# Softmax attention in a hybrid attention layer: heads taken one at a time, against pairs of heads on half arrays of TensorE

## The reference, cut to what matters

```python
# SWA (branch B, window 128, sink), WIN (branch A, window 512): banded_attention
s = einsum("bnqhgd,bnkhd->bnhgqk", qb, kw) * Dh ** -0.5 - slopes * rel     # window mask
p = masked_softmax(s, mask, sink);  o = einsum("bnhgqk,bnkhd->bnqhgd", p, vw)
# SEL (branch A, all 16 blocks of 64 keys are taken, so it is causal attention): sel_block
sc = einsum("bqhd,bqkd->bhqk", qi, kg) * scale - slopes * d
pr = masked_softmax(sc, d >= 0);        o = einsum("bhqk,bqkd->bqhd", pr, vg)
y_A = g0 * o_cmp + g1 * o_sel + g2 * o_win
# FGT (block two): forgetting_attention
logits = einsum("bhqd,bhkd->bhqk", qi, k32) * scale + ci - c               # causal mask
o = einsum("bhqk,bhkd->bhqd", softmax(logits), v)
```

## Time and profile before

| | |
|---|---|
| median of 3 runs | 2864.52 us (2863.51 to 2866.34) |
| the profiled execution | 2866.92 us, its span 2864.9 us |
| mean granted clock of TensorE | 0.951 of full |
| PE busy | 2675.0 us, 93% of the span, 12580 matmuls |
| DVE, ACT, POOL busy | 923.5, 818.3, 873.8 us |

### The profile page before, as it was taken

How to read it: one execution, slowest core, us unless ns; L and a number is a source line. 1 busy time by engine, 2 the same in 40 slices (tenths; PEclk the granted TensorE clock), 3 DMA queues, 4 the chain that set the end, 5 groups by cost and what they waited for, 6 DMA issues and landing times.

```text
span 2864.9 us, 30315 instructions
## 1 busy us (share of the span) xinstructions
PE 2675.0 (93%) x12580; PEld 2132.9 (74%) x12580; DVE 923.5 (32%) x1435; ACT 818.3 (29%) x1219; POOL 873.8 (31%) x492
## 2 busy tenths in 40 slices
PE   7799999999998999999998999698999999999896
PEld 5677778666686777787876777487888888888785
DVE  5213440233302544411147465504122222222423
ACT  4102441344322444422222333223211111111321
POOL 2112212444322111144632121234333232333633
PEclk8889999999998999999989999899999999999898
DMA  7001101100011000011212000120111111111111
GB/s 290 30 23 43 33 29 45 37 19 19 15 51 54 10 19 17 8 47 43 103 73 67 16 23 17 33 97 29 51 45 52 45 45 51 52 51 45 50 37 68
DMA packets 34440, 134.84 MB, mean 47 GB/s; under 512 B 3648, under 2 KB 4096, under 8 KB 32896
## 3 DMA queue, kind: packets, MB, share of 16 engines
q1 hardware_dynamic: 33984, 131.85, 13.3%
q10 hardware_dynamic: 320, 1.05, 0.1%
HBM read 123.45 MB, written 8.39 MB: 46 GB/s over the span
## 4 chain that ended last, share of the span: by engine, by line
PE 88%; DVE 5%; ACT 3%; POOL 2%; issue 2%; DMA 0%; POOLq 0%; SPq 0%; ACTq 0%; DVEq 0%
PE slot L659 55%; PE slot L705 12%; PE ps L887 4%; PE ps L858 3%; PE ps L836 2%; PE ps L737 2%; PE ps L920 1%; PE ps L911 1%; PE ps L924 1%; PE ps L937 1%; DVE cacc L2097 1%; PE ps L780 1%; POOL wlo L1500 1%; PE ps L763 1%; ACT zs L1226 0%
## 5 line engine op out<-in xcount | busy, mean ns | idle before, releaser
L659 PE MATMUL slot<-xhi,whi 128*128 128x512 f32 x2192 | 716.0, 408 | 57.6 <-ACT zs L1226 16.9
L659 PE MATMUL slot<-xlo,whi 128*128 128x512 f32 x2192 | 693.4, 398 | 0.0
L659 PE MATMUL slot<-xhi,wlo 128*128 128x512 f32 x2192 | 689.6, 396 | 0.0
L1500 POOL TENSOR_TENSOR wlo<-raw,whi 128x1024 fp32r<-128x1024 f32 (+1 forms) x169 | 429.0, 2539 | 835.1 <-ACT whi L1134 835.1
L659 PEld LDWEIGHTS slot<-xhi,whi 128*128 128x128 f32 x2192 | 406.5, 194 | 146.6 <-issue 65.3
L659 PEld LDWEIGHTS slot<-xlo,whi 128*128 128x128 f32 x2192 | 421.7, 192 | 92.2
L659 PEld LDWEIGHTS slot<-xhi,wlo 128*128 128x128 f32 x2192 | 421.3, 192 | 92.5
L1134 ACT ACTIVATE whi<-raw 128x1024 fp32r<-128x1024 f32 (+1 forms) x169 | 186.1, 1101 | 317.7 <-PE slot L705 174.1
L705 PE MATMUL slot<-uhi,whi 128*128 128x512 f32 x512 | 158.3, 390 | 0.0
L705 PE MATMUL slot<-ulo,whi 128*128 128x512 f32 x512 | 157.8, 389 | 0.0
L705 PE MATMUL slot<-uhi,wlo 128*128 128x512 f32 x512 | 157.6, 389 | 0.0
(11 more groups left out here) (315 smaller groups left out, 3079.1 us busy)
## 6 DMA issues: line engine op xcount, KB each, us to landing
raw<-wstream SPq DMA_DIRECT2D x129, 512.0 KB, 3.3
raw<-wstream SPq DMA_DIRECT2D x40, 640.0 KB, 3.9
ada<-wada SPq DMA_DIRECT2D x7, 1024.0 KB, 19.9
mm<-xT SPq DMA_DIRECT2D x2, 2048.0 KB, 9.8
ada<-wada SPq DMA_DIRECT2D x2, 2048.0 KB, 27.2
mm<-xT SPq DMA_DIRECT2D x8, 512.0 KB, 4.5
res_dram<-mm SPq DMA_DIRECT2D x8, 512.0 KB, 3.0
res<-res_dram SPq DMA_DIRECT2D x8, 512.0 KB, 6.7
```

The source lines that it names most:

```text
L659: o = mm_(outs[:, half * HALF:(half + 1) * HALF], w[b % 2][:, k_w, :], x[:, k_x, half * HALF:(half + 1) * HALF], start=first and j == 0, s ...
L1500: tt(flat(wlo[b % 2])[:, 0:n], (raw1 if b == 1 else raw)[:, 0:n], flat(whi[b % 2])[:, 0:n].bitcast(F32), ALU.subtract).then_inc(w_lo, 1)
```

## The change

Units become 64 **pairs**: heads 2t and 2t+1 for one block of queries (`pair`). The pair's keys are worked in pieces of at most 4 blocks (88 pieces in all). The queries of SEL, WIN and FGT come in the order 0, 7, 1, 6, 2, 5, 3, 4.

- Scores: head 0 of the pair on array rows 0 to 63 into the first bank of `ps4`, head 1 on rows 64 to 127 into the second, in turns. A second piece waits until the bias of the first has left the banks.
- DVE: bias for each head, one maximum over both heads, one factor for both, and now a multiplication of the exponentials by the factor before they are transposed (two `tensor_scalar` in `factor`, up to 128x1024 each).
- Product with V: V (64 columns) as weights, the transposed probabilities (128 columns) as the moving side; head 0 on array columns 0 to 63, head 1 on 64 to 127. The result has features on partitions and goes by one copy or addition to `yfm`. So `ytrans` is gone for A, B and FGT.
- The event `soft` is split into finer ones; only one pair is ahead of another: two buffers `ring` instead of three.
- `cmp` events weigh 1.0 and pauses 2.5 (10 pauses), where they weighed 2.0 and 5.0 beside heavier units; the last `cmp` step uses column groups too, and its gate is multiplied into the probabilities before.
- Retention: scores of even heads in one bank, of odd heads in the other, no `ordered`, no alternation.

```diff
+SOFT_WEIGHT = {"scores": 0.18, "turn_p": 0.12, "values": 0.28}     # times the piece's blocks
 def weight(ev):
-    if ev[0] == "soft":
-        u, first, n = ev[1:]
-        return 1.5 + sum(0.5 * unit(v)[4] for v in (u, u - 2) if first <= v < first + n)
+    if ev[0] in SOFT_WEIGHT:
+        return SOFT_WEIGHT[ev[0]] * piece(ev[1], ev[-1])[1]
+    if ev[0] in ("bias", "exp", "factor", "qsplit", "ksplit"):
+        return 0.0
...
+QORDER = (0, 7, 1, 6, 2, 5, 3, 4)
...
 def soft_events(first, n):
...
+    def scores(p):
+        rows = [("row", p, a) for a in range(2)] if pair(p)[0] == "FGT" and pair(p)[2] == 0 else []
+        return rows + [ev for c in range(pieces(p)) for ev in (("scores", p, c), ("bias", p, c))]
+    def products(p):
+        return [ev for c in range(pieces(p)) for ev in (("turn_p", p, 0, c), ("turn_p", p, 1, c), ("values", p, c))]
+    out += [("ksplit", first), ("qsplit", first), ("qsplit", first + 1)] + scores(first) + [("exp", first)]
+    for p in range(first, first + n):
+        this, ahead = products(p), []
+        if p + 1 < first + n:
+            ahead = scores(p + 1)
+            if p + 1 in KSPLITS:
+                out.append(("ksplit", p + 1))
+        if p + 2 < first + n:
+            out.append(("qsplit", p + 2))
+        out.append(("factor", p))
+        out.append(this.pop(0))
+        while ahead:
+            step = 1 if ahead[0][0] == "row" else 2
+            out += ahead[:step]
+            ahead = ahead[step:]
+            if ahead and len(this) > 1:
+                out.append(this.pop(0))
+        out += this[:-1]
+        if p + 1 < first + n:
+            out.append(("exp", p + 1))
+        out.append(this[-1])
...
+            def scores(p, c):                                       # PE
...
+                pe.wait_ge(s_biased, 2 * (PIECE0[p] + c))
...
+                for j, (q_, k_) in enumerate(((q_h, k_h), (q_h, k_l), (q_l, k_h))):
+                    for a in range(2):
+                        r = slice(a * DH, a * DH + DH)
+                        o = mm_(psb[a][:, 0:w], q_[r, :], k_[r, c0:c0 + w], start=j == 0, stop=j == 2)
...
+            def turn_p(p, a, c):                                    # PE
+                pe.wait_ge(s_scaled, 2 * p + a + 1)
+                pe.wait_ge(s_ptsb, turn_index(p, a, c))
...
+            def values(p, c):                                       # PE
+                pe.wait_ge(s_ptsb, turn_index(p, 1, c) + 1)
...
+                for j in range(n):
+                    for a in range(2):
+                        o = mm_(ps7[a * DH:a * DH + DH, 0:P], value_tile(p, a, b0 + j), ptr[:, a, j * P:(j + 1) * P],
+                                start=b0 + j == 0, stop=b0 + j == pair(p)[4] - 1)
...
+            def factor(p):                                          # DVE
...
+                dve.wait_ge(s_exp, 2 * p + 2)
...
+                link(v.tensor_scalar(d, d, TINY, None, ALU.max))
+                link(v.reciprocal(f, d))
+                if ph in ("SEL", "WIN"):
+                    g0 = 6 * t + (1 if ph == "SEL" else 2)
+                    link(v.tensor_tensor(f, f, gates[:, i, g0:g0 + 4:3], ALU.mult))
+                for a in range(2):
+                    r = ring[p % 2][:, a, 0:nb * P]
+                    v.tensor_scalar(r, r, fac[:, at_ + a:at_ + a + 1], None, ALU.mult).then_inc(s_scaled, 1)
...
+                elif ev[0] == "ymul":                               # DVE, instead of ytrans for A and B
+                    v.tensor_tensor(zs[n][:], yfm[:, n, :], zs[n][:], ALU.mult).then_inc(y_src, 1)
...
                 elif ev[0] == "mix":                                # DVE
                     split_wide(3, 0, 4, scy[:, 0, :])
                     split_wide(3, 2, 0, cu[:, 0, :])
-                    for t in range(2):
-                        g = TILE["yE%d" % t]
-                        wait_tile(dve, g)
-                        v.tensor_copy(pbuf[t][:], slot[g % 2][:]).then_inc(slot_free[g % 2], 1)
-                        wait_evacuated(dve, "yE%d" % t)
-                        v.tensor_copy(token[:, 0:1], token[:, 1:2]).then_inc(mix_src, 1)
-                    split_wide(3, 4, 2, pbuf[0][:])
+                    split_wide(3, 4, 2, yfm[:, 0, :])
```

More of the change, by code:

```diff
@@ L172, in soft_events @@
     out = []
-    for u in range(first, first + n + 3):
-        if u < first + n and u in KSPLITS:
-            out.append(("ksplit", u))
-        out.append(("soft", u, first, n))
+    def scores(p):
[24 more added lines that the diff above has]
+        out.append(this[-1])
     return out
@@ L299, in number_tiles @@
             g += 1
-        elif ev[0] == "mix":
-            tiles["yE0"] = g
-            g += 2
-    tiles["yE1"] = tiles["yE0"] + 1
     return tiles
@@ new lines, in forget_row @@
+            def forget_row(p, a):
+                t = pair(p)[1]
+                if (t, a) == (0, 0):
+                    pe.wait_ge(f_ci, 1)
+                    wait_evacuated(pe, "Ef")
+                pe.wait_ge(s_biased, 2 * PIECE0[p])
+                pe.wait_ge(f_cb, 2 * t + a)
+                h = 2 * t + a
+                for half in range(2):
+                    o = mm_(psb[half], t_("ident")[0:4, h:h + 1].to_broadcast([4, P]),
+                            ct[0:4, half * HALF:(half + 1) * HALF], start=True, stop=True)
+                o.then_inc(f_bc, 1)
@@ new lines, in bias @@
+            def bias(p, c):
+                ph, t, i, lo, nb = pair(p)
+                b0, n = piece(p, c)
+                w = n * P
+                dve.wait_ge(s_scores, PIECE0[p] + c + 1)
+                if p >= 2 and c == 0:
+                    dve.wait_ge(s_pt, turn_index(p - 1, 0, 0))
+                for a in range(2):
+                    dst = ring[p % 2][:, a, b0 * P:b0 * P + w]
+                    if ph == "FGT":
+                        if c == 0:
+                            dve.wait_ge(f_cb, 2 * t + 2)
+                        ins = v.scalar_tensor_tensor(out=dst, in0=psb[a][:, 0:w],
+                                                     scalar=ci[:, i, 2 * t + a:2 * t + a + 1],
+                                                     in1=cbs[a][:, b0 * P:b0 * P + w], op0=ALU.add, op1=ALU.subtract)
+                    else:
+                        o = (NB - 1 - i + lo + b0) * P
+                        ins = v.scalar_tensor_tensor(out=dst, in0=t_("dist", o, w), scalar=SLOPES[2 * t + a],
+                                                     in1=psb[a][:, 0:w], op0=ALU.mult, op1=ALU.add)
+                    ins.then_inc(s_biased, 1)
+                if c == pieces(p) - 1:
+                    at_ = 2 * (p % 2)
+                    nm = nmx[:, at_:at_ + 2]
+                    dve.wait_ge(s_biased, 2 * PIECE0[p + 1])
+                    ins = v.tensor_reduce(nm, ring[p % 2][:, :, 0:nb * P], AX, ALU.max, negate=True)
+                    if ph == "SWA":
@@ L1905, in stick, with outputs @@
+            def outputs(p):
+                ph, t, i, lo, nb = pair(p)
+                y = yfm[:, t, i * P:(i + 1) * P]
+                dve.wait_ge(s_out, PIECE0[p + 1])
+                if p == U_SWA:
+                    wait_tile(dve, TILE["yD1"])
+                if ph in ("SEL", "WIN"):
+                    v.tensor_tensor(y, ps7[:, 0:P], y, ALU.add).then_inc(s_norm, 1)
+                else:
+                    v.tensor_copy(y, ps7[:, 0:P]).then_inc(s_norm, 1)
             def stick(s):
@@ L2242, in tables @@
     d = c - p
-    r[:, 0:4 * P] = np.concatenate([np.where(d >= 0, np.exp(lg[h] * np.maximum(d, 0)), 0.0) for h in range(H)], 1)
+    r[:, 0:4 * P] = np.concatenate([np.where(d >= 0, np.exp(lg[h] * np.maximum(d, 0)), 0.0) for h in (0, 2, 1, 3)], 1)
     r[:, 4 * P:6 * P] = np.exp(lg[head][:, :, None] * (np.arange(P)[None, None, :] + 1)).reshape(P, 2 * P)
```

438 lines of the change are left out of this document (182 added, 256 removed).

## The result

The changed kernel takes 3002.97 us (median of 4 runs, 2999.88 to 3012.68) against 2864.02 us for the kernel before (2862.69 to 2866.34): a ratio of 1.049, 95% interval 1.0465 to 1.0515. The prediction said slower, 2896 us, with a range up to 2945. The direction was right; the loss is 139 us where 32 were forecast.

What follows compares the result with a forecast made beforehand. The kernel was taken as bound by PE, its work plus its gaps. Terms -110 (work) - 40 (old gaps) + 117 (chains) + 35 + 10 (other waits) + 20 (clock) made +32, so 2896 us, range 2820 to 2945.

Steps and rivals of the forecast that it cites:

- the idle time from chains: PE waiting for each pair's DVE and ACT chain: SEL 40, WIN 41, FGT 36, SWA 1, together 117 us.
- the clock: 2.7 us lost for each of 22 new gaps of 3 us and more: 60, so 20 more than now; bounds 0 and 60.
- PE's work: Saved on PE: products with V 48, scores 56, transposes 6, retention 6 us; the V products' new mode costs 18 back.
- The chain's length: From last score to first transposes of an eight-block pair in SEL: 8.1 us, 0.8 less with each block less.
- SWA has 3 to 5 parts per pair against 5.1: 1: In SWA, 3 to 5 dense parts per pair stand beside a chain of 5.1 us, so 1 us of idle time.
- Old gaps and copies: Most old gaps go, -40 us; waits for second score pieces and ACT's copies add 35, other small waits 10.
- The mix: Two copies and two tokens leave the DVE chain for which PE waits: gain 3 us.
- The signs for the stages: SEL with WIN 30 to 60 us longer than 297, SWA 15 to 25 shorter, FGT about the same.
- A: Rival: PE's work decides, gaps stay about as large, so faster: 2757 us, or 2800 to 2830 half covered; chance 0.27.
- B: Rival: row groups don't overlap with 512 columns in the scores, 56 us more, 2952 us; chance 0.10.
- C: Rival: clock stays at 1.2 GHz through most of SEL, WIN and FGT, 60 us more, 2956 us; chance 0.08.
- D: Rival: gain and gaps cancel within 0.2% over the whole kernel, 2865 us; chance 0.05.

Runs made afterwards that it cites:

- short_pool: Changed kernel with GpSimd's subtraction for the weights' low part cut to the first 128 columns in some dense blocks, leaving out right low parts there: 2988.3 us.
- no_scaling: Changed kernel without VectorE's two scalings of the exponentials; a pair's first transposes wait for its second exponential instead: 2901.2 us.
- weights: Changed kernel with other planner weights, so more dense parts stand between a pair's last scores and its first transposes; same work: 2888.5 us, 1.009 of before.
- tuned: Changed kernel with bias, maximum and scaling taken head by head and planner weights chosen by a small sum over its order: 2885.8 us.

## Why the prediction was right in direction and wrong in size

Two terms failed, both too small, and the same gaps pay both: the idle time from chains (117, measured 158) and the clock (20, measured 59.5). Step by step, forecast against measured, in us:

- **PE's work: held.** 48 + 56 + 6 - 18 and retention's 6 make 98 less on PE, against 89 less over the whole kernel (4 of them retention's). Overlap at 512 columns, the half price of the products and the 0.1 for a change of mode can stand.
- **The chain's length: held.** 8.1 us forecast, 8.0 measured.
- **The idle time from chains: too small.** 117 forecast, 158 measured (SWA 1 and 19, SEL with WIN 81 and 91, FGT 36 and 47.5). The step "SWA has 3 to 5 parts per pair against 5.1: 1" failed: it took every step of VectorE at the duration that it has alone. A hold by GpSimd of up to 2.7 us broke that; short_pool returned 6 of SWA's 19 us. no_scaling, where the transposes wait for the exponential alone, leaves 2.5 of the 19, so nearly all of it was set by what VectorE does behind the exponential. How much of the rest is the scaling itself and how much its queue the runs don't separate: an evacuation of a dense part of 1.23 us runs ahead of the denominator at 304.64 us.
- **Old gaps and copies: nearly right in sum.** For the four stages the forecast has 62 - 40 + 35 + 10 = 67 us beside the chain's, and measured are 230 - 158 = 72. But cmp gave 1 us of idle time (10.7 to 9.5), not the 9 taken, and its clock went from 0.81 to 0.78.
- **The clock: the term that failed most.** "60, so 20 more than all four stages lose now" put the whole loss of these stages after the change at 60 us; measured are 98 (38.6 before), so 59.5 more instead of 20, and 56 more in the kernel. The number of gaps of 3 us and more was right, 22 more (13 to 35). Two things were wrong. I let all of the present 40 us go with the old gaps, but at the starts of SWA and SEL and in cmp PE still waits as before (8.45, 5.15 and 5.69 us), and a stretch at 1.2 GHz stands behind FGT's first products with four rows (L932), as before. The stretches at these places (255 to 268.6, 893.3 to 930.8, 951.3 to 958.1 and 1674.9 to 1692.0 us) cost 21 us, where the same places cost 15 before. The other 77 us lie, but for a few, behind the chain's gaps, where I had 60: those of 2 to 3 us, which I didn't count, went from 9 to 20 in the kernel. That the rise of 59.5 equals my 60 is luck. The bound of 60 that I had named held the truth, but I kept the low end.
- **Small parts.** Retention gave 10 us by the medians and 13 in the profiled executions, not 6, most of it as clock. The mix gave 0, not 3: the two copies went, but one more step of VectorE there took 3.32 us instead of 1.22.

The forecast fell 107 us short, and 105 of them stand in the sums: 60 of idle time (41 of them the chain's), 36 of clock and 9 of work. The signs for the stages failed with it: SEL with WIN is 81 us longer, not 30 to 60, SWA 23.5 longer, not 15 to 25 shorter, and FGT 31 longer, not the same.

Of the rivals: A is refuted by the waits, B by the 0.23 us, D by the time. C was right in kind, more clock loss than forecast, but not in degree: 0.84 and 0.86 were measured within my 0.80 to 0.88, and C wanted under 0.75. B's price was also too high: its 56 us include 12 for fewer entries into the mode, which full overlap doesn't decide, so it stood for some 45. The range went wrong because terms that share one cause, the gaps, were taken as independent: the chain's excess of 41 and the clock's of 39 came together, and both follow from where dense work is placed. weights shows it from the other side: 106 us less of waiting brought 47 of clock.

A rule that I left out would have helped. The Trainium skill, "SBUF — State Buffer", Who interferes with whom, says that GpSimd and a VectorE instruction that uses both of its ports, or reads two tensors from SBUF, exclude each other for a whole instruction, and that a reduction never takes part. The traces here agree: the gate's product with two inputs (2.16 us in tuned), the 128x2 denominators (2.75 us in the changed kernel) and the scaling (3.27 us in tuned) were held. The 64 maxima of the changed kernel (L1898) lie within 5 ns of the shortest of their form, the 4 that start inside a GpSimd instruction too, and 128 denominators of the form 128x1 in tuned never were held, though 21 of them start inside one:

```profile
L1914 DVE TENSOR_SCALAR den<-den x128: 140/147/156, 266.5 to 1803.8; 128x1 f32<-128x1 f32 x128
```

The earlier trace rows has one step of this form and one free gate step. But the trace of before did show holds: 12 steps of its factors with two inputs (L1870, L1877) were held, for 17 us in sum, the longest beside the same subtraction:

```profile
291.55 2.96 POOL L1500 TENSOR_TENSOR wlo<-raw,whi 128x1280 fp32r<-128x1280 f32 x1 [9.95 <-ACT whi L1134]
...
291.85 2.67 DVE L1870 TENSOR_TENSOR den<-den,esk 128x1 f32<-128x1 f32 x1
```

There PE's waits for the step that uses the factor (`ytok`, L1852 and L1857) are 1.9 us in all, as three units were under way. So the change did not bring the holds (13 us in the changed kernel); it took away the slack that hid them, and the price of a factor, 0.67 us, was read from a free one.

On the clock, the Trainium skill, "TensorE: Matmul & The Clock Gate", HAM oscillation, tells of a kernel whose waits between groups of matmuls throw the clock back every time; this trace agrees, with 0.56 in the 6.8 us behind a gap of 5.69, and with 1.2 GHz for a part of the 5 us behind each of its 35 gaps of 3 us and more.

## What to carry to other kernels

When a change halves an engine's work but makes its order one item deep, compare the item's whole chain on the other engines with the work placed beside it, and charge each gap twice, once as idle time and once as clock. Then move the work, before you shorten the chain: four weights of a planner gave 114 us, a shorter chain 51. Where dense work is moved next to a chain on VectorE, what GpSimd does for that work comes along, and cutting its instructions into quarters let VectorE in between. And look for steps that take longer than their like also where nobody waits for them: the trace of before had them.

## What the runs showed of the hardware

- A VectorE step of 0.17 us took 2.75 us beside a GpSimd instruction of 2.90 us and ended with it; beside instructions of a quarter's length the longest scaling was 1.12 us instead of 3.27.
- Filling idle time with unused products raised the granted clock over cmp, SEL and WIN from 0.83 to 0.92.
- Two fp32r score matmuls on two row groups with 512 columns cost 0.23 us for both; 16 products on two column groups with 128 columns took 1.09 us.
